# First attention by pairs of heads: one rotary query tile for two heads, values of two heads with tokens on the partitions, and another order in the third layer's last head

## The reference

```python
# mla: 16 heads, ranks 512/512, nope 128, rope 64, value 128
c_q, c_kv, k_rope, gate = split(h @ mla_w_in)
q = (rmsnorm(c_q) @ w_uq).reshape(S, 16, 128 + 64)     # q_nope, q_rope
kv = (rmsnorm(c_kv) @ w_ukv).reshape(S, 16, 128 + 128) # k_nope, v
q_rope, k_rope = rope(q_rope, pos), rope(k_rope, pos)  # k_rope: one for all heads
s = (q_nope @ k_nope.T + q_rope @ k_rope.T) * 192 ** -0.5, causal
x = x + (softmax(s) @ v * silu(gate)) @ w_out
```

## Time and profile before

| | us |
|---|---|
| median of 3 runs | 2164.36 (2164.1 to 2164.68) |
| the profiled execution | 2164.45 |
| its span, first to last instruction | 2162.7 |
| busy in it: PE / DVE / ACT / POOL | 2142.0 / 1451.1 / 972.2 / 151.6 |

### The profile page before, as it was taken

How to read it: one execution, slowest core, us unless ns; L and a number is a source line. 1 busy time by engine, 2 the same in 40 slices (tenths; PEclk the granted TensorE clock), 3 DMA queues, 4 the chain that set the end, 5 groups by cost and what they waited for, 6 DMA issues and landing times. The chain is left out here.

```text
span 2162.7 us, 31059 instructions
## 1 busy us (share of the span) xinstructions
PE 2142.0 (99%) x10128; PEld 1787.6 (83%) x10128; DVE 1451.1 (67%) x2646; ACT 972.2 (45%) x1906; POOL 151.6 (7%) x173
## 2 busy tenths in 40 slices
PE   8999999999999999999999999999999999999999
PEld 6878888888888888888888888888888888887887
DVE  6677777777833568888888833676767676768432
ACT  5444444444432435555555633545453545355221
POOL 0100000000210010000000112200000000004000
PEclk9999999999999999999999999999999999999999
DMA  7322222223643623333333643532333233334742
GB/s 216 104 61 80 78 82 82 82 82 111 213 110 84 187 78 87 87 87 87 87 87 87 190 141 99 176 88 78 110 89 109 78 109 90 93 94 134 211 127 68
DMA packets 371484, 235.03 MB, mean 109 GB/s; under 512 B 5104, under 2 KB 345328, under 8 KB 371440
## 3 DMA queue, kind: packets, MB, share of 16 engines
q1 hardware_dynamic: 369312, 230.27, 37.2%
q10 hardware_dynamic: 2128, 4.19, 0.5%
HBM read 210.33 MB, written 24.12 MB: 108 GB/s over the span
## 5 line engine op out<-in xcount | busy, mean ns | idle before, releaser
L595 PE MATMUL pp<-act_hi,w_hi 128*128 128x512 f32 x2304 | 909.5, 395 | 15.2 <-DVE w_lo L569 11.6
L597 PE MATMUL pp<-act_hi,w_lo 128*128 128x512 f32 x2304 | 899.0, 390 | 0.0
L596 PE MATMUL pp<-act_lo,w_hi 128*128 128x512 f32 x2304 | 898.7, 390 | 0.0
L569 DVE TENSOR_TENSOR w_lo<-raw,w_hi 128x512 fp32r<-128x512 f32 x672 | 457.3, 707 | 292.3 <-ACT w_hi L560 289.2
L560 ACT ACTIVATE w_hi<-raw 128x512 fp32r<-128x512 f32 (+1 forms) x692 | 402.6, 618 | 335.2 <-PE pp L597 151.6
L595 PEld LDWEIGHTS pp<-act_hi,w_hi 128*128 128x128 f32 x2304 | 433.6, 188 | 103.8 <-DVE w_lo L569 11.0
L597 PEld LDWEIGHTS pp<-act_hi,w_lo 128*128 128x128 f32 x2304 | 433.2, 188 | 92.3
L596 PEld LDWEIGHTS pp<-act_lo,w_hi 128*128 128x128 f32 x2304 | 433.9, 188 | 84.8 <-issue 0.5
L1160 ACT ACTIVATE prob<-ps,minus,q_scale 128x512 f32<-128x512 f32 (+1 forms) x64 | 39.0, 615 | 97.8 <-DVE minus L1222 97.8
L595 PE MATMUL pp<-c_hi,w_hi 128*128 128x512 f32 x192 | 75.1, 391 | 0.2 <-DVE qn_lo L614 0.2
L596 PE MATMUL pp<-c_lo,w_hi 128*128 128x512 f32 x192 | 74.9, 390 | 0.0
(11 more groups left out here) (385 smaller groups left out, 2728.2 us busy)
## 6 DMA issues: line engine op xcount, KB each, us to landing
raw<-w_in SPq DMA_DIRECT2D x48, 1024.0 KB, 5.9
raw<-swa_w_in SPq DMA_DIRECT2D x36, 1024.0 KB, 5.6
raw<-mla_w_in SPq DMA_DIRECT2D x23, 1024.0 KB, 5.8
raw<-mla_w_out SPq DMA_DIRECT2D x16, 1024.0 KB, 6.5
raw<-swa_w_out SPq DMA_DIRECT2D x16, 1024.0 KB, 6.3
raw<-w_out SPq DMA_DIRECT2D x16, 1024.0 KB, 6.7
raw<-mla_w_ukv SPq DMA_DIRECT2D x16, 512.0 KB, 4.4
x_feature_major<-xT SPq DMA_DIRECT2D x8, 1024.0 KB, 8.6
```

The source lines that it names most:

```text
L569: q.eng.tensor_tensor(dst, raw_piece(tile, p), high, ALU.subtract).then_inc(s_lo, 1)
L595: q.eng.matmul(psum[:, :], wh, ah, start=start and n == 0, stop=False)
L596: q.eng.matmul(psum[:, :], wh, al, start=False, stop=False)
L597: last = q.eng.matmul(psum[:, :], wl, ah, start=False, stop=stop and n == PIECE // P - 1)
```

## The change

1. The rotary query columns of two heads (64 each) are loaded side by side with the even head's tile and multiplied as one ordinary tile of 12 matmuls, QR, in even units only; `multiply_stacked` is no longer used here. DVE turns both heads on 128 partitions in six operations, reading the bank directly; the halves are split into `q_stack_a` and `q_stack_b`.
2. The values of heads i-1 and i are computed in the odd unit i, with the normalized latent as stationary operand and the weights of both heads (256 columns) as moving operand: 48 matmuls of 256 columns. Tokens are then on the partitions, so the four transposes `vt` go; ACT and DVE split the result in four blocks with the rms as a scale per partition.
3. An even tile has three pieces, an odd one four. PE's order in an even unit is QR, KN, QN, pv; in an odd one values, KN, QN, pv. QN's split is last on DVE. The scores begin with the rotary part and wait for `V.qn_lo` after two matmuls. In unit 1, gate piece 0 comes ahead of the scores. The loop is over pairs of units.
4. Four more one-column products at the norms (`rstd_tok`).
5. Third layer: ACT makes the high parts of chunks 0 to 7, POOL of 8 to 11. The pieces of the next unit's first tile are split ahead of the key's norm. In unit 8, pieces 0 to 2 of the second output tile are split earlier.

```diff
-Y_WHOLE_GPSIMD = range(4, 12)
+Y_WHOLE_GPSIMD = range(8, 12)
...
+                if tile.odd:
+                    return [(second[:, :, nk:nk + V1], ukv[:, :, bass.ds((i - 1) * nk + NOPE, V1)], s_ukv),
+                            (first, uq[:, :, bass.ds(i * nq, NOPE)], s_raw[tile.slot]),
+                            (second[:, :, 0:nk], ukv[:, :, bass.ds(i * nk, nk)], s_ukv)]
+                return [(first[:, :, 0:nq], uq[:, :, bass.ds(i * nq, nq)], s_raw[tile.slot]),
+                        (first[:, :, nq:nq + ROPE1], uq[:, :, bass.ds((i + 1) * nq + NOPE, ROPE1)], s_ukv),
+                        (second, ukv[:, :, bass.ds(i * nk, NOPE)], s_ukv)]
...
             for b in range(NB):
                 q.eng.matmul(ps[2][:, b:b + 1], acc_q[:, b * P:(b + 1) * P], c("ones")[:, 0:1], start=True, stop=True)
+                q.eng.matmul(ps[2][:, NB + b:NB + b + 1], acc_kv[:, b * P:(b + 1) * P], c("ones")[:, 0:1], start=True, stop=True)
...  mla_T
+            def values():
+                q.eng.wait_ge(s_lo, up.count(VALUES[-1]))
+                for b in range(NB):
+                    o = ps[b // 2][:, b % 2 * 2 * V1:(b % 2 + 1) * 2 * V1]
+                    t_ = slice(b * P, (b + 1) * P)
+                    for p in VALUES:
+                        for n in range(2):
+                            s, cols, ch = up.piece_slot(p), slice(n * 2 * V1, (n + 1) * 2 * V1), RC + 2 * p + n
+                            last = products(q, o, (c_hi[:, ch, t_], c_lo[:, ch, t_]), (w_hi[:, s, cols], w_lo[:, s, cols]),
+                                            ch == RC, ch == 2 * RC - 1)
+            if isinstance(i, int) and i == 1:
+                q.eng.wait_ge(*q.at("V.gate", 0))
+                gate_piece(0)
             if attn:
-                q.eng.wait_ge(*q.at("V.kn_lo", i - 1))
-                q.eng.wait_ge(*q.at("V.qr_lo", i - 1))
+                q_stack = q_stack_a if odd else q_stack_b
+                q.eng.wait_ge(*q.at("V.qb_lo" if odd else "V.kn_ev", i - 1))
                 for b in reversed(range(NB)):
+                    q.eng.matmul(SCORE[b][:, 0:n], q_stack[:, t_], kr_hi[:, 0:n], start=True, stop=False)
+                    q.eng.matmul(SCORE[b][:, 0:n], q_stack[:, t_], kr_lo[:, 0:n], start=False, stop=False)
+                    if b == NB - 1:
+                        q.eng.wait_ge(*q.at("V.qn_lo", i - 1))
+                    m = products(q, SCORE[b][:, 0:n], (qn_hi[:, t_], qn_lo[:, t_]), (kn_hi[:, 0:n], kn_lo[:, 0:n]), False, True)
...
-                for b in range(NB):
-                    m = q.eng.transpose(pt[0][:, b * P:(b + 1) * P], vT[:, b * P:(b + 1) * P], c("ident"))
-                m.then_inc(*q.did("vt"))
...
-            if proj:
-                multiply_stacked(q, up, QR, pp[1], c_hi, c_lo, 0, True, True)
+            if proj and odd:
+                values()
+                up_piece(KN, pp[1])
+                q.eng.wait_ge(*q.at("V.gate"))
+                up_piece(QN, pp[0])
             elif proj:
+                up_piece(QR, pp[1])
+                up_piece(KN, ps[0])
+                up_piece(QN, ps[1])
...  mla_V, even unit
+                multiplied(q, up, QR)
+                q.eng.tensor_tensor(q_cos, pp[1][:, :], rope_table[:, :], ALU.mult).then_inc(*q.did("q_cos"))
+                for n in range(4):
+                    to, of = slice(n * HALF, (n + 1) * HALF), slice((n ^ 1) * HALF, ((n ^ 1) + 1) * HALF)
+                    q.eng.tensor_tensor(q_sin[to, :], pp[1][of, :], rope_sin[of, :], ALU.mult).then_inc(*q.did(f"q_sin{n}"))
+                q.eng.wait_ge(*q.at("V.q_sin3"))
+                q.eng.tensor_tensor(qr, q_cos, q_sin, ALU.add).then_inc(*q.did("qr"))
+                q.eng.tensor_tensor(kn, (pp[1] if odd else ps[0])[:, :], rstd_kv[:, :], ALU.mult).then_inc(*q.did("kn_ev"))
+                    sub_lo(q, q_stack_a[ROPE1:P, :], qr[0:ROPE1, :], q_stack_a[0:ROPE1, :], "qa_lo")
+                    sub_lo(q, q_stack_b[0:ROPE1, :], qr[ROPE1:P, :], q_stack_b[ROPE1:P, :], "qb_lo")
+                sub_lo(q, kn_lo[:, :], kn, kn_hi[:, :], "kn_lo")
+                sub_lo(q, qn_lo[:, :], (pp[0] if odd else ps[1])[:, :], qn_hi[:, :], "qn_lo")
+            if not odd:
+                next_lo(3)
...  stick_A
             if not proj:
-                hi(q, Tile("out3", 0, 1), 0)
+                for p in range(3):
+                    hi(q, Tile("out3", 0, 1), p)
...
+            hi_(6, 0, 1, 2, 3)
             if proj:
                 rms(pt[1], "T.k_norm", "k_root", d_th[:, :])
                 if nxt.phase == "out3":
                     exp_table()
-                    y_hi(q, 3, range(0, 4))
+                    y_hi(q, 3, range(0, 8))
                 copy_hi(q, d_k_hi[:, :], d_k[:, :], "k_hi")
-            hi_(6, 0, 1, 2, 3)
```

More of the change, by code:

```diff
@@ L103 @@
     "mla": {
[L104 to L107, removed]
+        "T": "s3 s2 s1 s0 t3 t2 t1 t0 values pv".split(),
+        "A": "exp3 exp2 exp1 exp0 pt_hi3 pt_hi2 pt_hi1 pt_hi0 tanh qa_hi qb_hi v_hi0 v_hi1 v_hi2 v_hi3 kn_hi qn_hi".split(),
+        "V": ("mask3 top3 minus3 mask2 top2 mask1 top1 mask0 top0 minus inv3 norm3 inv0 norm2 norm1 norm0 pt_lo3 "
+              "pt_lo2 pt_lo1 pt_lo0 gate v_lo0 v_lo1 v_lo2 v_lo3 q_cos q_sin0 q_sin1 q_sin2 q_sin3 qr kn_ev qa_lo "
+              "qb_lo kn_lo qn_lo y silu").split(),
     },
@@ L251, in __init__, with ups @@
         self.static_first = self.per == 0 or isinstance(i, int) and i == 0
+        self.odd = i % 2 == 1 if isinstance(i, int) else odd
+        self.pieces = PIECES - 1 if phase == "mla" and k == 1 and not self.odd else PIECES
+    def ups(self, p):
+        return 1 + PIECES - self.pieces if p == self.pieces - 1 else 1
     def loaded(self):
@@ L531, in raw_piece @@
             if tile.phase == "mla" and tile.k == 1:
[L532 to L535, removed]
+                first, second = up_parts(tile)
+                if tile.odd and p in VALUES:
+                    return second[:, 2 * p:2 * p + 2, NOPE:NOPE + 2 * V1]
+                if tile.odd:
+                    return [second[:, :, 0:NOPE], first][p - len(VALUES)]
+                return [first[:, :, NOPE:2 * NOPE], second, first[:, :, 0:NOPE]][p]
             if tile.phase == "out3":
@@ L538, in raw_piece, with split @@
             chunks = r[:, p * PIECE:(p + 1) * PIECE].rearrange("p (c n) -> p c n", n=P)
[L539 to L545, removed]
+            return chunks[:, :, ROPE1:P] if stacked(tile, p) else chunks
+        def split(buf, tile, p):
+            n = 2 * V1 if tile.phase == "mla" and tile.k == 1 and tile.odd and p in VALUES else P
+            return buf[:, tile.piece_slot(p), :].rearrange("p (c n) -> p c n", n=n)
         def hi(q, tile, p):
@@ L700, in attention_dmas @@
             unit(1, False)
-            with loop(q.eng, 2, units) as i:
-                unit(i, True)
+            if phase == "mla":
+                with loop(q.eng, 2, units - 1, 2) as i:
+                    unit(i, True, False)
+                    unit(i + 1, True, True)
+            else:
+                with loop(q.eng, 2, units) as i:
+                    unit(i, True)
             for k in range(2):
@@ L708, in attention_dmas @@
             if n == 1:
-                q.eng.wait_ge(*q.at("V.kn_lo", body=units - 1, phase=phase))
+                q.eng.wait_ge(*q.at("V.qn_lo", body=units - 1, phase=phase))
                 q.eng.dma_start(s_pos_i, positions.to_broadcast([P, S])).then_inc(s_pos, 16)
@@ L957, in in_A @@
                     q.eng.activation(fold_hi[:, :], c("fold"), ACT.Copy)
-                    for p in range(PIECES):
+                    for p in range(Tile("mla", 0, 1).pieces):
                         hi(q, Tile("mla", 0, 1), p)
@@ L2318, in silu_s @@
                 q.eng.scalar_tensor_tensor(d_silu_s[:, :], d_th[:, :], 1.0, d_gate, ALU.add, ALU.mult).then_inc(*q.did(step))
+            if not proj:
+                for p in range(2):
+                    lo(q, Tile("out3", 0, 1), p)
             if attn:
@@ L2322, in stick_V @@
             if not proj:
-                for p in range(2):
-                    lo(q, Tile("out3", 0, 1), p)
+                lo(q, Tile("out3", 0, 1), 2)
             if attn:
```

280 lines of the change are left out of this document (144 added, 136 removed).

## The result

The kernel after takes 2174.28 us (median of 6 runs, 2172.11 to 2175.61) beside 2164.59 of the kernel before: ratio 1.0041, 95% interval 1.0031 to 1.0051. It is slower by 9.7 us. The forecast was 2168.7, slower by 4.1, in a range of 2159 to 2173. The side was right, the size was not, and the time lies above the range.

What follows compares the result with a forecast made beforehand. The prediction took PE's issue as the bound, with DVE only 0.14 us ahead at t3. From 2164.45, +8.1 for the first layer and -3.7 for the third gave 2168.9, rounded down to 2168.7 us; range 2159 to 2173.

Steps and rivals of the forecast that it cites:

- PE's work: First layer, per pair of heads: rotary queries -0.94, values' transposes -0.88, values +0.24, in sum -1.58 us.
- Rival F: Values on PE cost more, since weight loads don't get shorter with 256 columns; no time given, chance 0.02.
- The wait at t3: First layer: PE waits at t3 for DVE's normalization, alternately 0.8 and 1.35 us, one of 3.3, some 19 in all.
- (c): DVE's mask3 is queued behind y and silu, so late: 0.17 us odd into even, 0.7 even into odd.
- The pair: Units 2 to 15, per pair: -1.58 + 0.8 + 1.65 = +0.87 us, period from 55.4 to 56.2.
- Rival C: Only the fixed part of the wait counts, mask3 on time in all units: 2160.1 us, chance 0.14.
- rival B: PE's sum alone decides, as DVE and ACT keep ahead: 2147.9 us, chance 0.08.
- Norms, +0.9: Once in the first layer: one-column products go from 8 to 16 entries with nothing beside them, +0.9 us.
- rival D: Waits at t3 bring PE's clock to 1.2 GHz: 2170.3 us at unit 1 alone, 2182 in every pair; chance 0.08.
- Unit 1, +1.7: Unit 1: wait of 3.3 us at t3, less saved PE work and old stalls of 0.5, makes +1.7.
- The third layer, -3.7: Third layer's last head: DVE's chain starts earlier, drops one piece and one slow scan, so pv comes 3.7 us earlier.
- Rival E: Third layer gains nothing, as POOL's and DVE's chains slow each other as before: 2172.3 us, chance 0.08.

Runs made afterwards that it cites:

- before_norms16: Kernel before with 16 one-column products of the token norms for 8, the added results unused: 2167.10 us, ratio 1.0006.
- the timed experiment: Kernel before with the third layer's part of the change alone (POOL's range, moved high and low parts): 2161.76 us, ratio 0.9983.
- after_again: Kernel after, unchanged, timed once more on another chip: 2173.45 us, ratio 1.0037 to the kernel before.
- before_no_vt: Kernel before without the four transposes of the values in each of 16 heads (output not the reference's): 2162.84 us, ratio 0.9988.
- norms16_again: Kernel before with 16 one-column norm products instead of 8, repeated on another chip for a second profile: 2166.74 us, ratio 1.0006.
- after_norm3_first: Kernel after with DVE's normalization of the probabilities ahead of the low parts of pieces 0 and 1: 2156.95 us, ratio 0.9958 to the kernel before.
- after_unit1_filled: Kernel after with gate piece 2 ahead of t3 and piece 3 behind it, in unit 1 alone: 2170.37 us, ratio 1.0022 to the kernel before.
- before_norms_late: Kernel before with the norms' 8 products behind gate piece 1: 2163.91 us, ratio 0.9996.

## Why the prediction was right in its side and wrong in its size

- **PE's work.** Confirmed within 0.1. With the waits at t3 out of the way the pair's period falls by 1.1, and 0.38 of the rest is the wait behind qn_lo. The price of 0.12 for 256 columns holds in the kernel after: its 48 matmuls of values in unit 3 go from 210.02 to 215.77. Rival F has no part in it.
- **The wait at t3.** Confirmed in kind, number and place: 16 waits where 15 and one in unit 16 were forecast, alternately short and long, one of 3.1 against 3.3. Counted by starts they are 0.63 and 1.16 against 0.8 and 1.35. The fixed part was too large: from mask3 to t3 the trace has 203.35 - 195.63 = 7.72 where I had 7.95. Of that 0.12 is the first low part, 5.78 behind mask3 and not 5.90, and 0.10 the way from DVE's end to PE, 0.05 here, the lower of my bounds. The part (c) was right: mask3 starts 9.6 behind q_cos, where I had 9.5. The four sines take 2.84, 0.71 each. The Trainium skill, VectorE: DVE Perf Modes, section "Two Vector instructions with no wait between them", has an instruction held until those ahead have finished when its input or output starts in another group of 32 partitions than the last one's; the trace agrees, with 0.71 for each sine and not 0.61.
- **The pair.** 56.15 against 56.2 forecast, 0.79 over the 55.36 of the kernel before, where the sum had 0.87. Rival C (2160.1) and rival B (2147.9) fall with it.
- **Norms, +0.9: this term failed.** "Nothing lies beside them" was right for the work, which is 0.9 (before_norms16's eight added entries at 0.11). In the profiled execution of after the place costs 4.1 (14.64 from the first product to unit 0's first, against 10.51), for the clock is at its lower level for most of 112 to 120. The step that failed is this one: the clock behind the wait at the norms was put at nothing. The prediction's list of the first layer's waits leaves out the 1.03 that stands in the earlier trace rows, and never brings it together with the windows of the earlier trace rows, where a fall follows a wait of 1.00: rival D was kept to the waits at t3.
- **Unit 1, +1.7.** The wait was right (3.2 by starts against 3.3); the 1.7 of clock behind it was rival D's "at unit 1 alone", with a chance of 0.08, and it came in every profiled execution that had this wait. The chance was too low: it rested on the wait of 2.15 at 1979 without a fall, and that was one execution. In four of the seven profiled executions with this wait the clock fell behind it.
- **Rival D in every pair** (2182) didn't come: the waits of 1.0 leave the clock at 1.00 throughout units 2 to 15.
- **The third layer, -3.7.** 3.7 by the timed experiment, 3.2 in the two traces. Rival E falls.

The sum against the profiled execution, by starts (measured: the trace of after against that of before):

| | forecast | measured |
|---|---|---|
| norms | +0.9 | +4.1, of it 3.2 clock |
| unit 1 | +1.7 | +3.1 |
| units 2 to 15 | +6.1 | +5.4 |
| unit 16 | -0.6 | +0.6 |
| ahead of the norms | 0 | -0.2 |
| first layer | +8.1 | +13.1 |
| third layer, to pv | -3.7 | -3.2 |
| behind pv | 0 | +0.4 |

So the missing term is the clock, at the norms and in unit 1: 3.2 and, of unit 1's excess, 1.4 make 4.6 of the 5.0. The rest is two misses that partly cancel, by luck: the seven pairs cost 0.7 less than forecast, and unit 16 cost 1.2 more. In unit 16 the wait at t3 is 0.94 by starts where I had 0.45, and the rest of its excess stays open. The clock's part varies from one execution to the next: after_again's profile shows 4 x (0.37 + 0.06) = 1.7 at the norms and 4 x (0.03 + 0.40) = 1.7 in unit 1, and its span was 1.3 shorter than that of the first. The range had room for one fall and should have reached to both.

What stays open: why the clock falls at one wait in one execution and not at the same wait in another, and whether the added products make the fall at the norms likelier.

## What to carry to other kernels

An order in an in-order queue is written for the chain that stands in it. When a change takes a step out (here vt and v_lo), ask again for each neighbour what it was placed for: two calls moved in DVE's queue turned +9.7 us into -9, and the same two calls moved in the kernel before cost 12.6. Where PE is busy all the time, find the slack of the next partner first; a cut in PE's queue beyond that slack is given back, and the partner's order, not its load of 65%, decides. And where a change makes PE wait, or leaves a wait standing ahead of narrow work, price the clock behind that wait at each such place: here 1.7 us behind a wait of 3.1, and up to 3.4 behind one of 1.0 that narrow products followed, the latter in some executions only. One trace in which the clock stayed up is not evidence that it will: look for the same wait in the traces of other kernels that share it.

## What the runs showed of the hardware

- A wait of 3.1 us of PE was followed in three of three profiled executions by some 1.7 us lost at the 1.2 GHz level (512 columns at 0.43 for 0.23). Waits of 0.5 to 1.0 us between stretches of full work, one in each of units 2 to 15, left it at 1.00 in the four profiled executions that have them.
- A wait of 2.15 us ahead of full work was followed by a fall in four of seven profiled executions (0.62 in the window 1976 to 1980 of before_no_vt), and in the kernel before the clock fell 13 us later instead, behind a wait of 1.00 at 1992.09 (0.57); in before_norms16 and norms16_again it fell behind neither.
- A wait of 1.0 with 8 or 16 one-column products and the 512-column full f32 product behind it was followed by a fall in some executions and not in others; the windows 112 to 116 read 0.50, 0.63, 0.63 and 0.71 where it came, and where the fall came ahead of it, as in after, the f32 product of 512 columns took 1.07 of start distance (113.47 to 114.54) against 0.54 at the full clock (111.99 to 112.53 in the kernel before). In after_again and after_norm3_first the fall came only behind that product.
- The mean granted clock of an execution, though it differs only in the third digit, goes with the time in most kernels here: 2167.6, 2169.6 and 2171.3 at 1.000, 0.999 and 0.998 in after_unit1_filled. In before_norms_late it doesn't (2164.3 and 2163.9 at 1.000 and 0.999). With effects of a few us it is worth a look before two kernels are compared by one profile each.
